# A hybrid encoder layer on one core: order of the gate work between heads in the gated linear attention stage

## The reference, cut to what matters

```python
lg = log_sigmoid(r @ w_gk + b_gk) / 16          # per head and direction, 128 channels
b  = cumsum(lg within a chunk)
q_t, k_t = q * exp(b), k * exp(-b)
A  = where(mask, q_t @ k_t.T, 0);  o = A @ v + q_t @ state
state = decay * state + k_hat.T @ v             # forward and backward scans, summed
o  = rmsnorm(o_f + o_b) * silu(g)
```

## Time and profile before

| | us |
|---|---|
| median of three runs | 3241.99 |
| the profiled execution | 3243.4 |
| its span | 3241.8 |
| TensorE busy in the span | 3032.2 (94%) |
| VectorE, ScalarE, GpSimd busy | 1706.0, 1518.9, 564.5 |
| GLA stage, from first VectorE work to last store issue | 550.9 to 974.6 |

### The profile page before, as it was taken

How to read it: one execution, slowest core, us unless ns; L and a number is a source line. 1 busy time by engine, 2 the same in 40 slices (tenths; PEclk the granted TensorE clock), 3 DMA queues, 4 the chain that set the end, 5 groups by cost and what they waited for, 6 DMA issues and landing times. The chain is left out here.

```text
span 3241.8 us, 51622 instructions
## 1 busy us (share of the span) xinstructions
PE 3032.2 (94%) x19370; PEld 2396.0 (74%) x19370; DVE 1706.0 (53%) x1733; ACT 1518.9 (47%) x1647; POOL 564.5 (17%) x732
## 2 busy tenths in 40 slices
PE   7999998899987799988885999999999999999998
PEld 5888886777776689967773777777777777777776
DVE  3101000544443299942337666666766766666665
ACT  4211111455543166631443565656656655566554
POOL 0038883012210000000101000111110001111100
PEclk9999998999998899999996999999999999999999
DMA  4324322232325300034436778888877787888874
GB/s 147 131 97 142 117 89 95 92 108 86 95 73 194 110 14 20 13 120 173 143 122 226 273 278 304 282 286 297 293 272 279 281 304 277 289 299 286 277 278 151
DMA packets 196508, 600.83 MB, mean 185 GB/s; under 512 B 15360, under 2 KB 45712, under 8 KB 196432
## 3 DMA queue, kind: packets, MB, share of 16 engines
q1 hardware_dynamic: 165952, 507.51, 43.9%
q0 software_dynamic: 21760, 74.99, 7.8%
q10 hardware_dynamic: 8720, 17.30, 1.5%
HBM read 522.33 MB, written 77.33 MB: 185 GB/s over the span
## 5 line engine op out<-in xcount | busy, mean ns | idle before, releaser
L1932 DVE TENSOR_TENSOR ex_w_lo<-ex_w_raw,ex_w_hi 128x2048 fp32r<-128x2048 f32 x384 | 879.7, 2291 | 451.5 <-ACT ex_w_hi L1887 451.5
L1887 ACT ACTIVATE ex_w_hi<-ex_w_raw 128x2048 fp32r<-128x2048 f32 x381 | 730.0, 1916 | 469.5 <-PE ex_ps_s L2019 469.3
L2019 PE MATMUL ex_ps_s<-ex_w_hi,ex_xS 128*128 128x512 f32 x2048 | 578.2, 395 | 0.0
L2019 PEld LDWEIGHTS ex_ps_s<-ex_w_hi,ex_xS 128*128 128x128 f32 x2048 | 375.9, 188 | 99.4 <-issue 26.3
L2019 PE MATMUL ex_ps_s<-ex_w_lo,ex_xS 128*128 128x512 f32 x1024 | 316.4, 390 | 0.0
L2019 PE MATMUL ex_ps_s<-ex_w_hi,ex_hidS 128*128 128x512 f32 x1024 | 307.9, 403 | 0.0
L1873 POOL DMA_INDIRECT y<-ex_ye_s,ex_rows_y x16 | 43.5, 2718 | 1147.4 <-DVE ex_ye_s L1975 1147.4
L2030 PE MATMUL ex_ps_p<-ex_w_raw,ex_xP 128*32 128x256 f32 x4096 | 236.1, 383 | 0.0
L109 PE MATMUL pj_ps_tok<-pj_w_hi,act_hl 128*128 128x512 f32 x560 | 219.5, 392 | 8.9 <-DVE pj_w_lo L406 8.9
L2019 PEld LDWEIGHTS ex_ps_s<-ex_w_lo,ex_xS 128*128 128x128 f32 x1024 | 192.2, 188 | 41.4
L111 PE MATMUL pj_ps_tok<-pj_w_hi,act_hl 128*128 128x512 f32 x560 | 218.6, 390 | 0.0
(11 more groups left out here) (293 smaller groups left out, 5117.7 us busy)
## 6 DMA issues: line engine op xcount, KB each, us to landing
ex_w_raw<-w_e_gate SPq DMA_DIRECT2D x128, 1024.0 KB, 11.3
ex_w_raw<-w_e_up SPq DMA_DIRECT2D x128, 1024.0 KB, 12.1
ex_w_raw<-w_e_down SPq DMA_DIRECT2D x128, 1024.0 KB, 8.7
proj_t<-pj_stage SPq DMA_DIRECT2D x60, 256.0 KB, 2.0
pj_w_raw<-w_cols ACTq DMA_DIRECT2D x7, 2048.0 KB, 9.2
z_w_raw<-w_z SPq DMA_DIRECT2D x16, 512.0 KB, 3.8
gate_logits<-gl_z_stage SPq DMA_DIRECT2D x32, 256.0 KB, 2.1
pj_w_raw<-x SPq DMA_DIRECT2D x10, 512.0 KB, 4.0
```

Of the source, the lines that this page charges most:

```text
L1887: act.activation(whl[0][:, j % NHL], raw[:, j % NRAW], ACT.Copy).then_inc(w_hi, 1)
L1932: dve.tensor_tensor(whl[1][:, j % NHL], raw[:, j % NRAW], whl[0][:, j % NHL].bitcast(F32), ALU.subtract).then_inc(w_lo, 1)
L2019: mm = pe.matmul(ps_s[:, s, c:c + 512], x(part, k), whl[w][:, j % NHL, kk, c:c + 512], start=k == 0 and part + w == 0, stop=k == 2 * PU - ...
```

## The change

At the end of a head, `exponentials(i+1, 0)` on ScalarE stands ahead of the "end" eviction and of `soft_ln(i+1, 1)`. On VectorE `log_gate`, `running_sum` and `center` of direction 1 move from the end of head i to behind `k_product` of head i+1, and the two query products move into the updates of direction 0. The opening of the stage is ordered likewise: `z_high(0, 0)` after three `gates_in`, the first logit evictions between the gate steps, mask and A set-up behind the first centring. SyncE issues the loads of gate weights, first logit weights, q and k ahead of `ph.start`.

```diff
-                ph.start(sp)
                 gate_weights(0)
                 load_z(0)
+                load_qk(0)
+                ph.start(sp)
                 sp.dma_start(A[:, 0], masks.rearrange("m p n -> p m n")).then_inc(const_in, 16)
-                load_qk(0)
...
-                    exponentials(i, 0)
                     z_at("start")
                     k_out(i, 0)
                     exponentials(i, 1)
...
                         z_at(("tile", t))
+                    if not last:
+                        exponentials(i + 1, 0)
                     z_at("end")
                     if not last:
                         soft_ln(i + 1, 1)
                     turned(NT - 1)
 
-                z_high(0, 0)
                 for n in range(2 * LIFT):
                     gates_in(0, n // LIFT, n % LIFT, n, n % 2)
+                    if n == LIFT - 1:
+                        z_high(0, 0)
                 soft_exp(0, 0)
+                soft_ln(0, 0)
+                z_evac(0, 0, 0, 0)
+                soft_exp(0, 1)
                 z_high(1, 1)
-                soft_ln(0, 0)
-                soft_exp(0, 1)
+                z_evac(1, 1, 1, 0)
+                exponentials(0, 0)
+                z_evac(2, 0, 2, 1)
                 soft_ln(0, 1)
-                for c in range(3):
-                    z_evac(c, c % 2, c, c // 2)
...
                     k_product(i)
-                    q_product(i, 0)
-                    between = {(0, 0): lambda: q_product(i, 1), (0, 2): lambda: low(0), (1, 1): lambda: None if last else low(1)}
+                    log_gate(i, 1)
+                    running_sum(i, 1)
+                    center(i, 1)
+                    between = {(0, 0): lambda: q_product(i, 0), (0, 2): lambda: low(0), (0, 6): lambda: q_product(i, 1),
+                               (1, 1): lambda: None if last else low(1)}
...
                             if t == 8:
                                 center(i + 1, 0)
-                            if t == 9:
-                                log_gate(i + 1, 1)
-                    if not last:
-                        running_sum(i + 1, 1)
-                        center(i + 1, 1)
 
                 dve.memset(starts[:], 1.0).then_inc(set_up, 1)
-                dve.wait_ge(const_in, 32)
-                dve.tensor_copy(mask[:], A[:, 0]).then_inc(set_up, 1)
-                dve.wait_ge(set_up, CR + 2)
-                dve.memset(A[:], 0.0).then_inc(set_up, 1)
+                dve.wait_ge(set_up, CR + 1)
                 dve.memset(starts[:, ::CH], 0.0).then_inc(set_up, 1)
-                dve.wait_ge(set_up, CR + 4)
                 z_low(0, 0)
                 negative(0, 0)
                 log_gate(0, 0)
                 negative(0, 1)
+                dve.wait_ge(set_up, CR + 2)
+                running_sum(0, 0)
                 z_low(1, 1)
-                running_sum(0, 0)
                 center(0, 0)
-                log_gate(0, 1)
-                running_sum(0, 1)
-                center(0, 1)
+                dve.wait_ge(const_in, 32)
+                dve.tensor_copy(mask[:], A[:, 0]).then_inc(set_up, 1)
+                dve.wait_ge(set_up, CR + 3)
+                dve.memset(A[:], 0.0).then_inc(set_up, 1)
+                dve.wait_ge(set_up, CR + 4)
                 heads(dve, body)
```

## The result

The changed kernel takes 3223.52 us (median of five, 3221.78 to 3226.66); the ratio to the kernel before, both timed side by side, is 0.9944, 95% interval 0.9930 to 0.9959. That is 18.5 us, where 29 were forecast: inside the stated range, but well short of the number. A second set of five runs gave 3225.76 us, ratio 0.9943 (0.9930 to 0.9957).

The account below looks back on a forecast made before the run. TensorE was taken to pace the GLA stage. Steps 16 plus opening 13 gave 29 us: 3214.4 us from the profiled execution's 3243.4, 3213 from the median 3242.0; range 3207 to 3228.

Parts of the forecast that it names:

- the forecast's own range: Total time of 3208 to 3219 us if the forecast itself holds; chance 0.68.
- rival (a): Only the steps win, the opening held by late data: 3226 us, or 3219 with half the opening; chance 0.14.
- signs: No key-product wait; 1.4 us eviction wait and 5.4 us to first update per head; logit product near 563, turn_k(0) near 584.
- the steps: Three passages from head to head on TensorE: 17.2 us extra cost, of which 16.0 would be won after contention.
- The opening: Start of the GLA stage, to the first turned keys: earlier loads, set-up and evictions win 13 us, bounds 7 and 15.
- contention: GpSimd's key product beside VectorE's query product and low(0): 0.4 us per step, 0 at best, 2 at worst.
- rival (c): Late direction 1 centring holds ScalarE's queue, stopping TensorE before "update 0,7": slower, 3249 us at 12 per step; chance 0.03.
- query product: On VectorE, 1.48 us, moved behind update 6 and covered by "update 0,7"; uncovered it would cost 1.5 us per head.
- table load: One more on ScalarE at each of three steps, 1.28 us, taken as hidden.

Follow-up runs that it names:

- scalar_half: The changed kernel with VectorE's order of before put back (direction 1's subtraction, scan and centring at a head's end): 3255.55 us, ratio 1.0037 to the kernel before.
- Opening_only: The kernel before with the whole new opening and its old loop over heads: 3239.05 us, ratio 0.9985.
- loads_only: The kernel before with only SyncE's first loads issued ahead of the start increments: 3241.97 us, ratio 0.9990.
- setup_only: The kernel before with only VectorE's set-up of mask and A moved behind the centring of direction 1: 3245.89 us, ratio 1.0005.
- changed_again: The changed kernel itself, run once more without edits: 3225.76 us.
- k1_on_vector: The changed kernel with direction 1's key product moved from GpSimd to VectorE behind update 5, second query product one place later: 3216.66 us, ratio 0.9913.
- zlow_later: The changed kernel with VectorE's weight split z_low moved from behind update 2 to behind update 4: 3222.77 us, ratio 0.9935.

## Why the prediction was right, and where its number was not

The range and the sign held. But 3223.5 lies outside 3208 to 3219, the forecast's own range, to which it gave 0.68. It lies near the 3226 of rival (a), and what (a) tells, an opening held by late data, did not happen; that the range held is in part luck. The changed kernel's new wait, 2.2 us of the updates for VectorE, is on none of the lines that the prediction named as signs. Step by step:

- "The steps cost ... 17.2 together": the steps gave 17.6 (the waits for the key product gone, 5.42 us from keys to update). The chain ran as worked out on ScalarE: table load 0.02 us after turned(8), kt 2.67 us later. scalar_half shows that ScalarE's half alone loses.
- The opening: first logit product at 563.6 (forecast 563.1), first keys at 584.9 (584.0), 12.3 us won (13). Opening_only, loads_only and setup_only show that it is no sum of single edits: each alone leaves another wait in force.
- The mis-sized term is contention: "I take 0.4", bounded by 2 us per step, and counted at three steps. The updates lost 1.6, 3.5, 3.4 and 2.4 us in four heads, 10.9 together (12.0 in changed_again). Three mistakes are in it.
- First, the stretched row of before was read as a factor (2.40 for 1.48), though it was a remainder: GpSimd's product began at 601.86 and took 2.93, so it ended at 604.79, and the query product begun at 603.75 ended 1.36 us later. By that reading a weight split begun 0.9 us into the product, as it was in head 0, loses 2.0 us; it lost 1.9, and 1.6 of them reached TensorE. The Trainium skill, "SBUF — State Buffer", § Who interferes with whom, had the rule: whoever issues first keeps the shared pair for the whole instruction, and the other blocks. It was cited and then used for GpSimd's delay, not for VectorE's.
- Second, head 0 was left out, though its product moved as well.
- Third, the slow clock behind the new wait was priced only in the rival (c). It makes the difference between 14.3 us in head 0 and 15.9 in heads 1 and 2, 1.6 us each. In head 3 1.5 of the 2.4 us are slow products: from 890.3 to 892.0 those of 512 columns follow each other at 0.43 us in place of 0.23, behind waits of 0.54 and 1.59 us. k1_on_vector has waits of 0.52 and 1.59 at the same place and full clock, and so has changed_again (0.51 and 1.59), so these 1.5 are not shown to come from the hold.
- k1_on_vector shows the size of both together: without the overlap the stage ends 29.9 us earlier than before. The prediction's sum without its contention term is 17.2 + 13 = 30.2. Of the 12.4 us won over the changed kernel, how much is the hold and how much a clock that varies between executions is settled only to the 1 to 2 us by which two profiles of one kernel differ in each part of the last head.
- A query product and the table load were costed at nothing. The query product behind update 6 stayed covered; so did the added load on ScalarE (3 more in the stage, and 1650 ScalarE instructions on the page against 1647).
- Rival (c) had the right place, VectorE late among the updates, with a wrong cause. The centring ended at 591.4, on time.

## What to carry to other kernels

When a move puts a GpSimd instruction beside VectorE, lay both on one time axis. In the rows here that began inside GpSimd's key product and took all their large inputs from SBUF, VectorE's instruction ended its own duration, less 0.1 to 0.2 us, after the end of that product (1.09 for 1.22, 1.36 for 1.48, 0.14 for 0.35). Price that for each instruction that could stand there, since moving one only hands the hold to the next. And check a saved wait against the engine behind it: of 1.1 us of waiting taken from TensorE 0.2 to 0.3 were left per head, and nothing in the total, until VectorE's work was thinned.

## What the runs showed of the hardware

- A VectorE tensor_scalar of 256 elements from SBUF to SBUF (0.35 us) is held for up to 3.14 us by GpSimd's product; scalar_tensor_tensor with one operand in PSUM (0.48 us) is not. The Trainium skill, "SBUF — State Buffer", § Who interferes with whom, lists tensor_scalar among the instructions that can take the shared pair; the traces agree.
- Which of the two began first by the profile does not always tell who is held: in head 3 the scaling's row begins 0.04 us ahead of the product's (888.75 and 888.79, again 882.30 and 882.34 in zlow_later) and is held until its end all the same.
- The clock behind equal waits is not fixed: after 2.20 us in head 0 full clock, after 2.18 us in heads 1 and 2 products of 256 columns at 0.21 us in place of 0.12. Even in one kernel it varies: behind a wait of 0.91 us in the last head the granted clock from 912 to 922 us is 0.83 in the changed kernel and 1.00 in changed_again. What decides between them stays open; in the last head it is worth 1 to 2 us either way.
- ScalarE's table at the entry of a hardware loop matters: entered with Exp's table and closed with Ln's, each turn had its load of 1.28 us at its head, ahead of the eviction of the keys; entered with Ln's, it stood behind that eviction, where ScalarE waited anyway (3.3 us ahead of 688.68 in the changed kernel). The number of loads per turn was the same.
